# Ten weight places before the joint attention, and modulation sums folded by transposes

## What is computed

```python
mod   = silu(c)     @ w_mod[l] + b_mod[l]      # w_mod[l]: 1024 x 6144, for l = 0 and 1
mod_c = silu(c_ctx) @ w_mod[l] + b_mod[l]
sh1, sc1, gt1, sh2, sc2, gt2 = split(mod, 6)
h = rms_norm(x) * (1 + sc1) + sh1              # and the same for the context
qa, ka, va, qb, kb, vb = split(h @ w_in_ab)    # 1024 x 1536
... joint attention, o @ w_out_ab, x = x + gt1 * o, experts, second layer, second block ...
```

## Time and profile before

| | us |
|---|---|
| median of 3 runs | 2652.04 (2651.12 to 2653.01) |
| profiled execution | 2647.32 |
| its span | 2645.5 |

### The profile page before, as it was taken

How to read it: one execution, slowest core, us unless ns; L and a number is a source line. 1 busy time by engine, 2 the same in 40 slices (tenths; PEclk the granted TensorE clock), 3 DMA queues, 4 the chain that set the end, 5 groups by cost and what they waited for, 6 DMA issues and landing times.

```text
span 2645.5 us, 27917 instructions
## 1 busy us (share of the span) xinstructions
PE 2396.6 (91%) x10390; PEld 1277.5 (48%) x10390; DVE 854.1 (32%) x1691; ACT 398.0 (15%) x964; POOL 87.5 (3%) x113
## 2 busy tenths in 40 slices
PE   5888997999999979997899999978979999779998
PEld 3435546333333334444544444434748644566843
DVE  2446514333333345453322222234621002371101
ACT  1004312101000111042101110111410001241000
POOL 0110001000000001100000000000000000000000
PEclk8888897999999989998899999999989999899999
DMA  7456333999999961203599999963214442403442
GB/s 287 159 182 271 130 125 132 380 422 422 421 421 421 421 259 64 80 16 119 226 421 422 422 422 422 422 264 116 75 64 146 157 151 87 159 1 127 159 143 72
DMA packets 148931, 609.34 MB, mean 230 GB/s; under 512 B 9584, under 2 KB 19824, under 8 KB 99568
## 3 DMA queue, kind: packets, MB, share of 16 engines
q1 hardware_dynamic: 145072, 592.94, 57.3%
q10 hardware_dynamic: 2480, 10.10, 0.9%
q0 software_dynamic: 1296, 5.17, 0.5%
HBM read 594.02 MB, written 14.16 MB: 230 GB/s over the span
## 4 chain that ended last, share of the span: by engine, by line
PE 76%; DVE 10%; DMA 7%; issue 3%; ACT 2%; POOL 1%; SPq 1%; another core or an unknown queue 0%; DVEq 0%; ACTq 0%; POOLq 0%
PE psum L2188 16%; PE psum L1828 11%; PE psum L2380 8%; PE psum L2393 8%; PE psum L2201 7%; PE psum L2248 6%; PE psum L1763 3%; PE psum L2298 3%; DMA rows<-in_w 3%; DMA ring<-in_w 2%; PE psum L1820 2%; PE psum L2162 1%; POOL rstd L403 1%; PE psum L2338 1%; PE psum L1952 1%
## 5 line engine op out<-in xcount | busy, mean ns | idle before, releaser
L1828 PE MATMUL psum<-ring,hT 128*128 128x512 f32 x832 | 375.0, 610 | 13.7 <-issue 6.5
L2188 PE MATMUL psum<-ring,arena 128*64 128x512 f32 x1536 | 346.1, 598 | 5.9 <-ACT arena L758 3.7
L1828 PEld LDWEIGHTS psum<-ring,hT 128*128 128x128 f32 x832 | 160.4, 196 | 213.0 <-issue 204.7
L1441 DVE TENSOR_TENSOR arena<-arena,psum 128x512 f32<-128x512 f32 x204 | 140.2, 687 | 292.7 <-PE psum L2201 290.6
L2188 PEld LDWEIGHTS psum<-ring,arena 128*64 128x64 f32 x1536 | 112.8, 137 | 232.5 <-issue 226.8
L2393 PE MATMUL psum<-ring,arena 128*128 128x512 f32 x512 | 220.3, 592 | 3.2 <-DVE arena L1657 3.2
L2380 PE MATMUL psum<-hT,ring 128*128 128x256 f32 x1024 | 221.5, 379 | 1.3 <-DVE hT L1522 1.3
L2380 PEld LDWEIGHTS psum<-hT,ring 128*128 128x128 f32 x1024 | 194.4, 190 | 28.0 <-DVE hT L1522 1.7
L2201 PE MATMUL psum<-arena 128*128 128x512 f32 x408 | 184.2, 601 | 1.7 <-DVE arena L1504 1.7
L2248 PE MATMUL psum<-ring,arena 128*64 128x512 f32 x768 | 171.9, 596 | 7.1 <-DVE arena L1492 7.1
L2393 PEld LDWEIGHTS psum<-ring,arena 128*128 128x128 f32 x512 | 97.1, 190 | 125.5 <-issue 121.5
(11 more groups left out here) (281 smaller groups left out, 2196.6 us busy)
## 6 DMA issues: line engine op xcount, KB each, us to landing
ring<-in_w SPq DMA_DIRECT2D x288, 1024.0 KB, 10.7
rows<-in_w SPq DMA_DIRECT2D x96, 1024.0 KB, 11.9
ring<-in_w_ff SPq DMA_DIRECT2D x64, 1024.0 KB, 5.2
ring<-in_w_mod SPq DMA_DIRECT2D x48, 1024.0 KB, 11.5
ring<-in_w_in_c SPq DMA_DIRECT2D x12, 1024.0 KB, 6.3
ring<-in_w_in SPq DMA_DIRECT2D x12, 1024.0 KB, 8.1
x_rows<-arena ACTq DMA_DIRECT2D x1, 8704.0 KB, 32.0
hT<-x_rows SPq DMA_DIRECT2D x16, 512.0 KB, 14.7
```

Of the source, the lines that this page charges most:

```text
L1441: dve.tensor_tensor(f, f, bank, ALU.add).then_inc(v_free, 1)
L1828: inst = pe.matmul(bank, hT[:, k, P * m:P * m + P], w[k], start=k == 0, stop=k == KB - 1)
L2188: inst = pe.matmul(out[64 * e:64 * e + 64, :], xgT[:, b, k, 64 * e:64 * e + 64], m, start=k == 0, stop=k == KB - 1)
```

## The change

Two edits.

1. **Ten places until the joint attention.** The list of places before the attention becomes `EARLY_PLACES`: the six of `ring`, two in `gate` (places 8 and 9) and two in `arena[:, 12288:16384]` (places 10 and 11). Just before the attention's chunks (on SP before the loads of mod block 10, on PE before `attention_ab`) the list goes back to the six of `ring`.
2. **Folds by transposes.** `folded` transposes each group of 128 columns of `mrow` (four transposes of 128 x 128, filling the bank) in place of the matmul with `fold`; VectorE then sums the four parts with a `tensor_reduce` into the new buffer `mod_sum` (which frees the bank) and adds the bias in an operation of its own, with a step semaphore after it.

```diff
 RING = 6
 EXPERT_RING = 8
+EARLY_PLACES = [0, 1, 2, 3, 4, 5, 8, 9, 10, 11]
@@ Slots
-        self.size, self.at, self.count, self.user = RING, 0, 0, {}
+        self.places, self.at, self.count, self.user = EARLY_PLACES, 0, 0, {}
     def resize(self, size):
-        self.size, self.at = size, 0
+        self.places, self.at = list(range(size)), 0
     def take(self):
-        slot = self.at % self.size
+        slot = self.places[self.at % len(self.places)]
@@ build
+        mod_sum = sb("mod_sum", [P, 8]).rearrange("p (k r) -> p k r", r=2)
         def slot_at(i):
-            return ring[:, i, :] if i < RING else rows[...]
+            if i < RING:
+                return ring[:, i, :]
+            if i < 8:
+                return rows[:, 2 * (i - RING):2 * (i - RING) + 2, :].rearrange("p a n -> p (a n)")
+            if i < 10:
+                return gate[:, i - 8, :, :].rearrange("p a n -> p (a n)")
+            return arena[:, 12288 + CHUNK * (i - 10):12288 + CHUNK * (i - 9)]
@@ with_bias (VectorE)
-                return dve.tensor_tensor(modT[l][:, bass.ds(4 * c, 4), :], bank[:, 0:8].rearrange("p (k r) -> p k r", r=2), bias, ALU.add)
+                parts = bank.rearrange("p (k j n) -> p k n j", k=4, j=4)[:, :, 0:2, :]
+                dve.tensor_reduce(mod_sum, parts, AX, ALU.add).then_inc(v_free, 1)
+                dve.wait_ge(v_free, so_far(v_free))
+                return dve.tensor_tensor(modT[l][:, 4 * c:4 * c + 4, :], mod_sum, bias, ALU.add)
@@ mod_columns (VectorE)
-                    with_bias(l, x, bank).then_inc(v_free, 1)
-                    dve.wait_ge(v_free, so_far(v_free))
+                    with_bias(l, x, bank).then_inc(v_step, 1)
+                    dve.wait_ge(v_step, so_far(v_step))
@@ folded (PE)
-                    inst = pe.matmul(out[:, 2 * j:2 * j + 2], sums[:, P * j:P * j + P], co("fold"), start=True, stop=True)
+                    inst = transpose(out[:, P * j:P * j + P], sums[:, P * j:P * j + P])
@@ PE's program
             heads(3, lambda c: all4, turn_ab, modulate=True)
+            slots.resize(RING)
             attention_ab()
```

More of the change, by code:

```diff
@@ L272, in slot_at @@
         def slot_at(i):
-            return ring[:, i, :] if i < RING else rows[:, 2 * (i - RING):2 * (i - RING) + 2, :].rearrange("p a n -> p (a n)")
+            if i < RING:
[5 more added lines that the diff above has]
+            return arena[:, 12288 + CHUNK * (i - 10):12288 + CHUNK * (i - 9)]
         gate_diag = [arena[:, o:o + 2048].rearrange("p (w k n) -> p w k n", w=2, k=KB) for o in (10240, 16384)]
@@ L281, in build @@
         zeroed = sem("zeroed")
-        loaded = [sem(f"loaded{i}") for i in range(EXPERT_RING)]
+        loaded = [sem(f"loaded{i}") for i in range(max(EARLY_PLACES) + 1)]
         used = sem("used")
@@ L891, in with_bias @@
             def with_bias(l, c, bank):
-                bias = pa("b_mod", at=6 * KB * l, width=6 * KB)[:, bass.ds(4 * c, 4), None].to_broadcast([P, 4, 2])
-                return dve.tensor_tensor(modT[l][:, bass.ds(4 * c, 4), :], bank[:, 0:8].rearrange("p (k r) -> p k r", r=2), bias, ALU.add)
+                bias = pa("b_mod", at=6 * KB * l, width=6 * KB)[:, 4 * c:4 * c + 4, None].to_broadcast([P, 4, 2])
+                parts = bank.rearrange("p (k j n) -> p k n j", k=4, j=4)[:, :, 0:2, :]
+                dve.tensor_reduce(mod_sum, parts, AX, ALU.add).then_inc(v_free, 1)
+                dve.wait_ge(v_free, so_far(v_free))
+                return dve.tensor_tensor(modT[l][:, 4 * c:4 * c + 4, :], mod_sum, bias, ALU.add)
             def mod_columns(l, c):
@@ L2209, in moe @@
                 tallies = {v_done: 2 * per_pair, a_done: 6, picks: 2}
-                tallies.update({c: 24 // EXPERT_RING for c in chunk_in})
+                tallies.update({c: 24 // EXPERT_RING for c in chunk_in[:EXPERT_RING]})
                 slots.resize(EXPERT_RING)
```

## The result

The changed kernel takes 2612.64 us (median of 4 runs, 2610.28 to 2621.14), the kernel before in the same comparison 2651.58 us; the ratio is 0.9859 with a 95% interval of 0.9833 to 0.9885. Two later comparisons of the same kernel gave 0.9872 (0.9852 to 0.9892) and 0.9880 (0.9861 to 0.9899), medians 2617.43 and 2613.63. So 32 to 39 us were gained; the first comparison stands at the high end.

The account below looks back on a forecast made before the run. PE was taken to wait before the attention for weights loaded too late for want of places, then run at low clock. 1.5 + 6.6 + 1.8 + 6.3 + 3.1 + 6.2 = 25.5 us less gave 2626.5 us, range 2618 to 2633.

Parts of the forecast that it names:

- What bounded the kernel: Ends of column blocks before the attention: PE waits for weights loaded too late; first tiles start 6.6 and 6.3 us earlier.
- The clock of the first tiles: First tiles of c = 1 and 2: full clock, 7.03 us each, gaining 1.8 and 3.1 us.
- The start of the attention behind its last products: Last products before the joint attention: from 197.02, the attention starts at 209.5 in place of 215.70, gaining 6.2 us.
- Folds: Transposes at 0.51 us a set gain 1.5 us at the start (bounds 0.5 to 2.0), 0 in the gaps.
- the clock behind the folds: Last four sets before the attention: no clock effect on the attention was priced; the attention was carried over at 0.
- the second tiles: Second tiles of c = 1 and 2: expected to stay as slow, 10.13 us, behind idle PE; no gain.
- the clock being kept in the gaps: Rival for the gaps before the second tiles: both run in 7.03 us, 2 x 3.1 us more, 2620; chance 0.10.
- After the attention: Stage with six places again: shorter folds but longer waits for weights, 0 gained; last set's wait grows to 2 to 4 us.
- The rest: Everything later, where nothing is changed: only shifted, no gain or loss.
- 1 (clock lost elsewhere): First tiles and late wait after the attention at low clock: gain of 15.5 to 22 us, 2630 to 2636; chance 0.17.
- 3 (places don't help): Before the attention: loads still late, only the last set's wait goes; gain about 12 us, 2640; chance 0.05.
- 4 (slower): Remaining 2295 us: average clock falls from 0.96; at 0.945 the kernel takes about 2661 us; chance 0.02.

Follow-up runs that it names:

- narrow_last: The changed kernel with the last four sets before the joint attention folded as before, by narrow matmuls; median 2616.97 us.
- places_only: The kernel before with the ten places alone, folds left as narrow matmuls with sum and bias in one operation; 2626.77 us, ratio 0.9894.
- warm_gaps: The changed kernel with the last fold in the gaps of c = 1 and 2 done nine times over; median 2610.02 us.
- late_places: The changed kernel with ten places also from the joint attention to the last modulation product; 2602.05 us, ratio 0.9819.
- places8: The changed kernel with eight early places, the two of `arena` left out; median 2629.75 us.
- after_fourth: The changed kernel unaltered, run again in the same rounds as two kernels with added transposes; median 2613.63 us.
- probe_transposes: The changed kernel with 160 further transposes into an unused bank just before the joint attention; one trace, no median, the transposes took 17.68 us.

## Why the prediction was wrong, point by point

**What bounded the kernel: right.** The waits were for weights, they went with the places, and VectorE was next, at the copy of the first product bank: 1.06 and 1.34 us of idle PE, and the tiles at 38.02 us behind the first of c = 0 for 37.9 forecast. The stretch gave 6.5 for 6.6. The clock of the first tiles: 1.7 and 3.0 for 1.8 and 3.1. The start of the attention behind its last products: 12.51 us (175.67 to 188.18) for the 12.5 of the prediction (197.02 to 209.5).

**Folds: right in kind, small in size at the start.** A set of four transposes takes 0.48 us of 1.91 for four (0.51 forecast), VectorE's pair 0.43 (0.41), the gaps gave nothing. The start gave 2.2 us for 1.5, just outside its bounds of 0.5 to 2.0: the two sets of folds gave 1.6 and 0.4, and the products between them lost nothing (5.27 us from start to start for 5.42). Three further traces of the kernel had 2.6, 1.7 and 2.0 against the first of before, and 4.1 to 4.9 against the second, whose rows there took longer (the norm's 9.02 us for 7.39); a difference of some tenths can't be read here.

**The step that failed: the clock behind the folds.** The prediction noted that 4.64 us of narrow folds were followed by half clock, and asked about transposes only for the two gaps. It didn't ask the same for the last four sets before the attention and, with that, for the attention's first 12 us, which it carried over unseen at 0. There the folds are followed by less than 1 us of idle PE, and the attention's first eight rows run at half clock behind narrow folds and at full clock behind transposes (3.55 to 3.78 us and 1.99, in all seventeen traces). The attention gained 2.9 us in the first pair: 0.9 by those rows, and 2.0 because the clock was also kept behind the wait for ScalarE, which the kind of fold doesn't decide (seven of twelve traces with transposes lost it there). narrow_last puts the price of narrow folds at 1.3 us of the attention. The prediction also kept the second tiles at 10.13, "as slow", where they came down to 9.29 and 9.23: 1.8 us in sum. This isn't due to the kind of fold, since places_only had 8.96 and 8.65, and against the second trace of before (9.51 and 9.67) it is only 0.7.

The Trainium skill, page "TensorE: Matmul & The Clock Gate", Part 4: PE-mode transpose, says that a transpose doesn't count as busy PE for the clock in the way that a matmul does. The probe speaks against it for float32 transposes of 128 x 128 on this chip: 17.68 us of nothing but transposes at 1.00, and the measurement decides. The prediction had put 0.10 on the clock being kept in the gaps, in part on that rule's word. That rival didn't happen: 4.7 us of idle PE remained in each gap. Where most of the wait was filled with transposes (warm_gaps), the clock was kept.

**After the attention**: 0 forecast, 0.6 measured. The last set's wait grew from 0.97 to 3.39 us, within the 2 to 4 that were named. But the prediction read only that wait; the 4.62 us before 315.21 and the new 4.88 before 295.98 belong to the same full stream, and it is that stream, not PE, that sets the length of the stage: late_places took 11.8 us off it.

**The rest** was taken as fixed: 2295.3 us before and after. It isn't; the one stretch that no edit touches varies by 6.7 us in one kernel. And the distance between the profiled execution and the median, 4.7 us before, was carried over as if it were a property of the program; it was 1.3 after. The measured median lies 13.9 us below the forecast of 2626.5. These two are 8.3 of them, the two clock terms 4.7 and the start 0.7; the remaining differences are small. So the larger part of the miss is drift between executions that no experiment tied to the change, and neither it nor the clock step alone would have left the range of 2618 to 2633. A range of 15 us for a kernel whose runs alone spread over 11 (2610.28 to 2621.14), around a sum that put these clock terms at 0, was too narrow.

The rivals: 1 (clock lost elsewhere), 3 (places don't help) and 4 (slower) didn't happen. In places8 the slow stretch behind the projection (2301.8 us against 2295.4 before) shows that a loss there of some 6 us occurs, and not of 25; one trace can't say that the edit caused it.

## What to carry to other kernels

When DMA is full at the end of a block and idle in its middle, count the chunks that the block's end consumes at once and give the ring that many places, if dead buffers can hold them: ten for two and eight here; with eight places 5.5 us of the gain were lost by the attention. When an operation on PE is exchanged for another, price also the clock of what follows it: the matmuls with two moving columns kept PE busy here and were still followed by half clock, and the next stage paid. Where PE must wait for another engine anyway, redoing a transpose into its own bank kept the clock here and made the next tile 2.2 us shorter at each of two waits of 4.7 us. But follow such a gain to the end of the chain: this one was gone at the projection, behind a stage that waits for its weights, and stayed only where that wait had been removed. And before a forecast of 25 us, trace the kernel twice: what differs between two traces of one kernel (here 6.7 us) is the least width of the range.

## What the runs showed of the hardware that I had not expected

- 160 transposes of 128 x 128 in float32 ran at a granted clock of 1.00 and took 17.68 us, 0.11 us each. 80 matmuls of 128 x 128 by 2 columns (160 rows) at the same place fell to 0.50 and took 33.94 us; PE was busy all through both.
- The same wait of 2.97 us for ScalarE, behind the same eight rows at full clock, was followed by full clock in five traces and by a fall in seven (the attention 0.6 to 1.9 us longer), with the same kind of folds in all twelve.
- A sum over four parts of a PSUM bank, 32 numbers a partition read with strides and eight written, takes 0.19 us on VectorE, 0.02 more than an addition of eight.
- The same 8726 rows of PE took between 2100.2 us (after_fourth) and 2115.9 (probe_transposes) of busy time in traces of kernels that are alike there, while VectorE's stayed at 694.9 to 695.2 us.
